# Second half of the embedding projection as the first unit of the kernel, its result kept in DRAM

## The reference

```python
n1 = rmsnorm(h); z = n1 @ w_in                     # q | k | v | u | g_a | g_b
m = sigmoid(g_a) * (attention(q, k, v) @ w_branch_a) + sigmoid(g_b) * (pool(u) @ w_branch_b)
h = h + m @ w_out
h = h + square(relu(rmsnorm(h) @ w_up)) @ w_down
gate = sigmoid(rmsnorm(h) @ w_ple_gate)
e = rmsnorm(p @ w_ple_proj)                         # the embedding: p is 320 x 256, an input
h = h + gate * e
y = rmsnorm(h)
```

## Time and profile before

| | |
|---|---|
| median of the runs | 1684.16 us (1683.98 to 1684.43, three runs) |
| span of the profiled execution | 1682.3 us |
| median less that span | 1.9 us |
| PE busy | 1657.2 us, 99% |
| DVE busy | 853.4 us, 51% |
| ACT busy | 670.3 us, 40% |
| POOL busy | 83.9 us, 5% |
| PE's share of the chain that ended last | 97% |
| moved by DMA | 252.48 MB, mean 150 GB/s |

### The profile page before, as it was taken

One profiled execution on the slowest core, in us unless ns is written; L12 is line 12 of the kernel. 1 busy time (PEld: TensorE's weight loads), 2 busy tenths in 40 slices (PEclk: granted clock), 3 DMA queues, 4 the chain that ended last, 5 costly groups with the idle time before them and its releaser, 6 DMA issues.

```text
span 1682.3 us, 29192 instructions
## 1 busy us (share of the span) xinstructions
PE 1657.2 (99%) x11286; PEld 1649.0 (98%) x11286; DVE 853.4 (51%) x1180; ACT 670.3 (40%) x973; POOL 83.9 (5%) x76
## 2 busy tenths in 40 slices
PE   7999999999999999999999999999999999999996
PEld 7999999999999999999999999999999999999996
DVE  7577544444445556443344443344433544555765
ACT  6355534333333444443334432234333344444442
POOL 3034000000000003000000000000000300000000
PEclk9999999999999999999999999999999999999998
DMA  7533544444444444444444444444444444444431
GB/s 283 172 116 126 198 149 149 149 148 150 149 149 156 150 150 151 150 150 150 150 150 150 150 150 150 149 149 148 146 147 149 148 147 149 144 149 151 147 125 62
DMA packets 37816, 252.48 MB, mean 150 GB/s; under 512 B 5264, under 2 KB 6544, under 8 KB 8336
## 3 DMA queue, kind: packets, MB, share of 16 engines
q1 hardware_dynamic: 35136, 245.59, 41.1%
q10 hardware_dynamic: 2640, 6.35, 1.0%
HBM read 248.65 MB, written 3.27 MB: 150 GB/s over the span
## 4 chain that ended last, share of the span: by engine, by line
PE 97%; DVE 2%; ACT 1%; DMA 0%; issue 0%; POOL 0%; DVEq 0%; SPq 0%; POOLq 0%; ACTq 0%
PE acc L405 32%; PE acc L407 32%; PE acc L406 32%; PE s_ps L457 1%; DVE w_lo L809 0%; DMA h<-in_x 0%; PE o_ps L435 0%; PE t_ps L444 0%; DVE sumsq L874 0%; DVE h L1159 0%; ACT xa_hi L601 0%; DVE xa_lo L865 0%; ACT w_hi L580 0%; POOL prob_t L344 0%; PE m_ps L419 0%
## 5 line engine op out<-in xcount | busy, mean ns | idle before, releaser
L580 ACT ACTIVATE w_hi<-raw 128x1024 fp32r<-128x1024 f32 x462 | 487.4, 1059 | 882.6 <-PE acc L407 878.9
L405 PE MATMUL acc<-xa_hi,w_hi 128*128 128x320 f32 x2112 | 655.5, 310 | 9.4 <-DVE xa_lo L865 9.0
L406 PE MATMUL acc<-xa_lo,w_hi 128*128 128x320 f32 x2112 | 653.3, 309 | 0.0
L407 PE MATMUL acc<-xa_hi,w_lo 128*128 128x320 f32 x2112 | 653.2, 309 | 0.0
L809 DVE TENSOR_TENSOR w_lo<-raw,w_hi 128x1024 fp32r<-128x1024 f32 x462 | 550.6, 1232 | 19.1 <-ACT w_hi L580 18.8
L405 PEld LDWEIGHTS acc<-xa_hi,w_hi 128*128 128x128 f32 x2112 | 397.2, 188 | 10.4 <-DVE w_lo L809 9.6
L406 PEld LDWEIGHTS acc<-xa_lo,w_hi 128*128 128x128 f32 x2112 | 397.2, 188 | 0.2
L407 PEld LDWEIGHTS acc<-xa_hi,w_lo 128*128 128x128 f32 x2112 | 397.1, 188 | 0.0
L405 PE MATMUL acc<-xb_hi,w_hi 128*128 128x320 f32 x1280 | 395.8, 309 | 0.0
L406 PE MATMUL acc<-xb_lo,w_hi 128*128 128x320 f32 x1280 | 395.5, 309 | 0.0
L407 PE MATMUL acc<-xb_hi,w_lo 128*128 128x320 f32 x1280 | 395.5, 309 | 0.0
(11 more groups left out here) (157 smaller groups left out, 938.9 us busy)
## 6 DMA issues: line engine op xcount, KB each, us to landing
raw<-in_weights SPq DMA_DIRECT2D x229, 1024.0 KB, 4.8
h<-in_x SPq DMA_DIRECT2D x4, 640.0 KB, 8.0
h<-in_x ACTq DMA_DIRECT2D x1, 2560.0 KB, 11.2
raw<-in_weights SPq DMA_DIRECT2D x4, 512.0 KB, 9.1
out_y<-h ACTq DMA_DIRECT2D x2, 800.0 KB, 3.5
out_y<-h ACTq DMA_DIRECT2D x1, 640.0 KB, 3.0
bias<-in_alibi SPq DMA_DIRECT2D x1, 512.0 KB, 11.3
p_raw<-in_p_in ACTq DMA_DIRECT2D x1, 320.0 KB, 2.7
```

The source lines that it names most:

```text
L405: nc.tensor.matmul(out, w_hi[:, at:at + P], x_hi[:, m * T:(m + 1) * T], start=k == 0, stop=False)
L406: nc.tensor.matmul(out, w_hi[:, at:at + P], x_lo[:, m * T:(m + 1) * T], start=False, stop=False)
L407: mm = nc.tensor.matmul(out, w_lo[:, at:at + P], x_hi[:, m * T:(m + 1) * T], start=False, stop=k == depth - 1)
L580: nc.scalar.activation(w_hi[:, dst:dst + HALF], raw[:, src:src + HALF], ACT.Copy).then_inc(hi_done, 1)
```

## The change

The unit of embedding chunks 8 to 15 moves from before the last block to the very front; it is called U_FIRST, and all the x units have an index one higher. Its eight chunks go to all eight PSUM banks. DVE evicts the even ones and ACT the odd ones to `e_first`; POOL squares and adds them from there; then SP writes `e_first` to DRAM (`spill`), and ACT reads it back into `e` after the merge. Its weights come in three pieces, p on ACT's queue with the gains behind it. x comes in eight parts instead of four, half of unit 1 after the second part and the other half after the fifth. PE runs eight matmuls on a cleared piece of `w_lo` first. The splits of units 2 and 3 stand after the third and the ninth square.

```diff
-SPLIT_AFTER = (6, 12)
+SPLIT_AFTER = (2, 8)
+U_FIRST = 0
+U_KV = U_FIRST + 1
+X_PARTS = 8
+WARM = 8
+FIRST_PIECES = ((0, HALF // 2), (HALF // 2, HALF), (HALF, UNIT))
...
+        first_bank = (*acc, s_ps, t_ps, o_ps, m_ps)
+        spill = nc.dram_tensor("e_spill", (P, KA * T), F32, kind="Internal").ap()
... SyncE
-            nc.sync.dma_start(g_all[:, :], gains).then_inc(gains_in, 16)
-            load_half(0, 0, first_in[0])
+            for (a, z), done in zip(FIRST_PIECES, (quarter_in, first_in[0], raw_in[0])):
+                load_part(U_FIRST, a, z, done)
             load_x(0)
             load_x(1)
-            load_half(0, 1, raw_in[0])
-            load_x(2)
-            load_x(3)
-            load_half(1, 0, first_in[1])
-            load_half(1, 1, raw_in[1])
-            load(2, 2)
+            load_part(1, 0, HALF, first_in[1])
+            for i in range(2, 5):
+                load_x(i)
+            load_part(1, HALF, UNIT, raw_in[1])
+            for i in range(5, X_PARTS):
+                load_x(i)
+            load(2, stored(2), 2)
...
-            load(3, 3)
+            load(3, stored(3), 3)
+            sp.wait_ge(ev_dve, KA // 2)
+            sp.wait_ge(ev_act, KA // 2)
+            nc.sync.dma_start(spill, e_first[:, :]).then_inc(spilled, 16)
... GpSimd
             nc.gpsimd.memset(odd_sum, 0.0).then_inc(xodd, 1)
+            def embedding_square(n, src, square):
+                if n:
+                    pool.wait_ge(e_add, n)
+                nc.gpsimd.tensor_tensor(square[:, :], src, src, ALU.mult).then_inc(e_s, 1)
+                pool.wait_ge(e_s, n + 1)
+                nc.gpsimd.tensor_tensor(esum[:, :], esum[:, :], square[:, :], ALU.add).then_inc(e_add, 1)
+            pool.wait_ge(ml, 2)
+            for c in range(KA):
+                if c % 2:
+                    pool.wait_ge(ev_act, c // 2 + 1)
+                else:
+                    pool.wait_ge(ev_dve, c // 2 + 1)
+                embedding_square(c, e_first[:, tt(c)], e_sq_first)
             for n in range(KD // 2):
                 pool.wait_ge(xs, 2 * n + 2)
... TensorE
+            pe.wait_ge(warm, 1)
+            for n in range(WARM):
+                mm = nc.tensor.matmul(s_ps[:, :], w_lo[:, 3 * HALF:3 * HALF + P],
+                                      w_lo[:, 3 * HALF:3 * HALF + 512], start=True, stop=True)
+            mm.then_inc(warmed, 1)
+            for t in range(TILES):
+                o, k = divmod(t, KP)
+                if t in (0, TILES // 4, TILES // 2):
+                    pe.wait_ge(lo_done, 4 * t // TILES + 1)
+                if t < KP:
+                    pe.wait_ge(pf_l, k + 1)
+                ... three matmuls of w_hi, w_lo with pf_hi, pf_lo into first_bank[o]
+            pe.wait_ge(ev_dve, 2)
+            pe.wait_ge(ev_act, 2)
...
-            embed(U_P1, C_P1)
... ScalarE
+            for k in range(KP):
+                nc.scalar.dma_start(p_first[:, tt(k)], p_in[:, tt(k)]).then_inc(p_in_first[k], 16)
+            nc.scalar.dma_start(g_all[:, :], gains).then_inc(gains_in, 16)
+            split_first(0)
+            for k in range(KP):
+                act.wait_ge(p_in_first[k], 16)
+                nc.scalar.activation(pf_hi[:, tt(k)], p_first[:, tt(k)], ACT.Copy).then_inc(pf_h, 1)
+            split_first(1)
+            split_first(2)
+            evict_first(1)
             act.wait_ge(gains_in, 16)
+            for c in range(0, 4):
+                high(c)
+            evict_first(3)
+            split(1, 1, [0])
+            evict_first(5)
+            for c in range(4, 8):
+                high(c)
+            evict_first(7)
+            for c in range(8, 10):
+                high(c)
+            split(1, 1, [1])
+            for c in range(10, KD):
+                high(c)
...
+            ahead(U_KV + 1, U_KV + 1)
             act.wait_ge(xl, KD)
...
+            act.wait_ge(spilled, 16)
+            nc.scalar.dma_start(e[:, KA * T:KD * T], spill).then_inc(e_back, 16)
... VectorE
+            nc.vector.memset(w_lo[:, 3 * HALF:3 * HALF + 512].bitcast(F32), 0.0).then_inc(warm, 1)
...
+            split_first(0)
+            for k in range(KP):
+                dve.wait_ge(pf_h, k + 1)
+                nc.vector.tensor_tensor(pf_lo[:, tt(k)], p_first[:, tt(k)], pf_hi[:, tt(k)],
+                                        ALU.subtract).then_inc(pf_l, 1)
+            split_first(1)
+            split_first(2)
+            def evict_first(c):
+                small_ready(dve, used, full, U_FIRST, 0, c)
+                nc.vector.tensor_copy(e_first[:, tt(c)], first_bank[c][:, 0:T]).then_inc(ev_dve, 1)
+            evict_first(0)
+            dve.wait_ge(gains_in, 16)
+            for c in range(0, 4):
+                low(c)
+            evict_first(2)
+            dve.wait_ge(warmed, 1)
+            split(1, 1, [0])
+            evict_first(4)
+            for c in range(4, 8):
+                low(c)
+            evict_first(6)
+            for c in range(8, 10):
+                low(c)
+            split(1, 1, [1])
+            for c in range(10, KD):
+                low(c)
...
-            embed(U_P1, 1)
```

More of the change, by code:

```diff
@@ L86, with stored @@
 C_MLP = C_P0 + KD // 2
-C_P1 = C_MLP + (FB - 1) * 2 * KF
-C_LAST = C_P1 + KD // 2
+C_LAST = C_MLP + (FB - 1) * 2 * KF
 C_GATE = C_LAST + 2 * KF
-assert RAW == 4 and not any(c % BANKS for c in (C_U, C_POOL, C_MIX, C_OUT, C_P0, C_MLP, C_P1, C_LAST, C_GATE))
+assert RAW == 4 and not any(c % BANKS for c in (C_U, C_POOL, C_MIX, C_OUT, C_P0, C_MLP, C_LAST, C_GATE))
+STORED_FIRST = U_LAST - 1
+def stored(u):
+    return STORED_FIRST if u == U_FIRST else u - 1 if u < U_LAST else u
 KX = 3 * CHUNK + SEQ
@@ L167, in encoder_step @@
         vx = h[:, KA * T + NPAIR * KX:KA * T + 2 * NPAIR * KX]
+        with ExitStack() as first:
+            e_first = sb("e_first", KA * T, F32, first)
         with ExitStack() as early:
@@ L374, in _ @@
                     probabilities(U_U - U_STEP - 1 + c)
[L377 to L383, removed]
+            for c in range(KA):
+                pool.wait_ge(taken, C_P0 + c + 1)
+                embedding_square(KA + c, e[:, tt(c)], e_sq)
         @block.tensor
@@ L459, in step @@
                     mm.then_inc(at_qk, 1)
+            pe.wait_ge(warm, 1)
[9 more added lines that the diff above has]
+                    pe.wait_ge(pf_l, k + 1)
+                at = t * P
+                out = first_bank[o][:, 0:T]
+                nc.tensor.matmul(out, w_hi[:, at:at + P], pf_hi[:, k * T:(k + 1) * T], start=k == 0, stop=False)
+                nc.tensor.matmul(out, w_hi[:, at:at + P], pf_lo[:, k * T:(k + 1) * T], start=False, stop=False)
+                mm = nc.tensor.matmul(out, w_lo[:, at:at + P], pf_hi[:, k * T:(k + 1) * T],
+                                      start=False, stop=k == KP - 1)
+                if t % 8 == 7:
+                    mm.then_inc(used, 1)
+                elif k == KP - 1:
+                    mm.then_inc(full, 1)
+            pe.wait_ge(ev_dve, 2)
+            pe.wait_ge(ev_act, 2)
             for u in range(U_KV, U_STEP):
-                unit(u, u % 2, u, u % BANKS, KD, xa_hi, xa_lo,
-                     ready=(lambda o, k: pe.wait_ge(xl, k + 1)) if u == 0 else None)
-                if u == 2:
+                unit(u, u % 2, u - U_KV, (u - U_KV) % BANKS, KD, xa_hi, xa_lo,
+                     ready=(lambda o, k: pe.wait_ge(xl, k + 1)) if u == U_KV else None)
+                if u == U_KV + 2:
+                    pe.wait_ge(ev_act, KA // 2)
                     pe.wait_ge(xadd, KD // 2)
@@ L481, in _ @@
             for u in range(U_STEP, U_POOL):
-                unit(u, u % 2, u, u % BANKS, KD, xa_hi, xa_lo)
+                unit(u, u % 2, u - U_KV, (u - U_KV) % BANKS, KD, xa_hi, xa_lo)
                 step(u - U_STEP)
@@ L617, in _ @@
             root(0, sumsq, r)
-            for u in range(2, U_STEP):
+            for u in range(U_KV + 2, U_STEP):
                 ahead(u, u)
-            act.wait_ge(taken, U_Q)
+            act.wait_ge(e_add, KA)
+            act.wait_ge(taken, U_Q - U_KV)
             act.wait_ge(kv_cache, 32)
@@ L861, in _, with split_first, evict_first, low @@
             dve.wait_ge(ul, 2)
-            split(0, 0, [0])
-            for c in range(KD):
+            def split_first(i):
+                a, z = FIRST_PIECES[i]
+                dve.wait_ge(hi_done, i + 1)
+                nc.vector.tensor_tensor(w_lo[:, a:z], raw[:, a:z], w_hi[:, a:z], ALU.subtract).then_inc(lo_done, 1)
+            split_first(0)
[5 more added lines that the diff above has]
+            split_first(2)
+            def evict_first(c):
+                small_ready(dve, used, full, U_FIRST, 0, c)
+                nc.vector.tensor_copy(e_first[:, tt(c)], first_bank[c][:, 0:T]).then_inc(ev_dve, 1)
+            def low(c):
                 dve.wait_ge(xh, c + 1)
```

102 lines of the change are left out of this document (58 added, 44 removed).

## The result

The changed kernel takes 1692.40 us (median of 4 runs, 1691.63 to 1693.37) against 1684.07 us for the kernel before, measured beside it: a ratio of 1.0049 [1.0037, 1.0061], 8.3 us slower. The profiled execution has a span of 1689.8 us against 1682.3 us, so the traces have 7.5 us to explain. Left out of all ratios are one run of the kernel before (2731.59 us) and one of experiment 5 (3214.82 us), whose mean granted clock was far lower (0.557 and 0.936) than that of the others (0.993 to 0.997).

What follows compares the result with a forecast made beforehand. TensorE was taken to bound the whole, VectorE the first 18 us. U2 at 32.7 - 18.48 before - 7.17 for the moved unit - 0.4 wait + 0.8 clock = +7.4 us: median 1691.6 us, range 1682 to 1696.

Steps and rivals of the forecast that it cites:

- VectorE with GpSimd beside it: From 10.9 us, VectorE's two-SBUF-operand operations alternate with sixteen GpSimd squares and sums: 0.98 us per xa_lo instead of 0.474.
- U2: Start of the second unit on x (index 2 in the changed kernel): 18.48 us before, forecast 32.7, break-even 26.05.
- the head: Kernel start until x can be split: last weight piece landed at 8.2 us, its low part done at 10.5 us.
- rival 1: At xa_lo: VectorE keeps its pace, GpSimd adds less than 1.75 us in all; 1682.3 us, chance 0.15.
- VectorE's chain alone: VectorE's work from 10.5 us to U2 without GpSimd: 13.8 us, putting U2 at 24.3 us.
- rival 2: VectorE reaches U2 at 24.3 us, but late GpSimd sums delay unit 3 to 41 us; 1692.1 us, chance 0.07.
- rival 3: At xa_lo, turns exclude each other for whole instructions: 1.27 us per chunk instead of 0.98; 1696 us, chance 0.06.
- rival 4: At the start, no turns and first weights landing 2 us earlier, U2 at 22 us; 1680 us, chance 0.07.
- The clock: TensorE's clock may fall to 1.2 GHz in its pause before U2: 0.8 us counted, range 0 to 1.6.
- the wait for GpSimd's sum: At the norm's sum: TensorE's 0.4 us wait for GpSimd goes, as the odd sums end near 44 us.
- The first unit's clock: At the start: low clock costs 1.6 us in the first unit, nothing while VectorE opens the next at 16 us.
- After U2: Unit 3 split at 36 to 38 us, odd sums ended near 44; from there the old order, shifted.

Runs made afterwards that it cites:

- experiment 5: Changed kernel, embedding squares and sums on GpSimd waiting until K and V are evicted, weights of U2 split before the squares of x; 1680.09 us, ratio 0.9977.
- Experiment 3: Kernel before, with only sixteen extra GpSimd squares and sums on otherwise unused tiles near the start; 1693.52 us, ratio 1.0056.
- experiment 1: Changed kernel with GpSimd's loop over the embedding moved behind the sums of x and the clearing of q; 1683.29 us, ratio 0.9993.
- experiment 2: Changed kernel with each early GpSimd square and sum replaced by a memset of about its length, which reads nothing; 1681.40 us, ratio 0.9986.
- experiment 4: Changed kernel with dummy TensorE matmuls, 18 before the second half of unit 1 and 14 before U2; 1690.55 us, ratio 1.0039.
- experiment 6: Changed kernel with embedding chunks 0 to 3 squared early and 4 to 7 moved behind the clearing of q; 1687.42 us, ratio 1.0019.
- experiment 7: Changed kernel with dummy matmuls in both pauses and three before each further chunk of unit 1's second half; 1690.20 us, ratio 1.0037.

## Why the prediction was right

**VectorE with GpSimd beside it: right, and the whole of the sign.** U2 was forecast at 32.7 us and came at 32.15. The pair of a square and a sum takes 2.01 us where the row at 647 us gave 1.96. Experiment 3 produces the cost without the change, experiment 1 the change without most of the cost, and experiment 2 shows that GpSimd's reads make it. What it came early is the head: ScalarE began the last piece at 7.51 us and its low part was done at 9.83, not at 10.5. (The working has two slips here that go the other way: 5.89 less 4.6 is 1.29, not 1.1, and 8.2 + 1.19 + 1.22 is 10.61.) From there to U2 it took 22.32 us, where 22.2 were forecast.

**No turns (rival 1)** is what experiments 1 and 2 make by hand: 1683.3 and 1681.4 us, where 1682.3 was worked out; U2 at 24.98 and 23.47 us, where VectorE's chain alone was put at 24.3. Experiment 2 is that chain with the earlier head. Experiment 1 has two things more that the chain left out: the sums of x on GpSimd meet U2's halves, and the first unit at the lower clock holds VectorE for 1.06 us. Experiment 5, with neither and with no square sums before the halves, reaches 22.16. **GpSimd always loses (rival 2)** falls with the 0.84 to 1.04 us of xa_lo. **A whole-instruction lock (rival 3)** would have put the pair near 2.5 us (0.47 + 0.80 twice); it is 2.01. The section of the Trainium skill that the prediction names there gives the exclusive lock for the shared ports in general, and spells "the whole instruction" out for VectorE's two-port modes; for these two-input operations the runs show less than that. **A shorter head (rival 4)** was right in its direction by 0.7 us, not 2.

**The clock was mis-sized.** 0.8 us was counted, half of 1.6; U2 lost 1.53, nearly the upper bound. The reason given, the pause before U2, isn't what the runs point to: in experiment 1 TensorE stands 1.62 us before U2 after a dense stretch and the clock stays, and in experiment 4 it falls in the thin stretch of unit 1 with the pauses filled. But within the longer pause of the changed kernel, 2.95 us, it fell too, and no run keeps the pause of 2.10 us before U2 and fills the thin stretch alone, so that pause's own part stays open.

**The sum's closeness is luck.** It said +7.4, and +7.46 came. Its terms are off by -0.55 us (U2), +0.73 (the clock) and -0.17 (the wait for GpSimd's sum moved the norm's sum by 0.57, the listed 0.41 with the restart), and these cancel: U2 +13.67, the clock +1.53, the wait -0.57 make the +14.63.

**The first unit's clock was counted at nothing, which held only in some executions.** The prediction said that a low clock there costs nothing while VectorE opens the next unit. In experiments 1 and 6 it costs VectorE 1.06 us, by way of ScalarE's first eviction, which stands ahead of the chunks of x. In the changed kernel's profile the first unit ran at 0.147 us a matmul, so nothing of it shows there; the eight warm-up matmuls are the same in all of these.

**After U2: right.** ScalarE split unit 3 at 35.4 to 37.4 us (36 to 38 forecast for its first half), the odd sums of x ended at 42.86 (44), and TensorE waited for neither. The covers named for the edits counted at nothing held: no wait of TensorE for evictions before unit 1, none of ScalarE for the weight load behind the spill, no wait for the read-back, and no change at 1318 us but the missing unit.

The median came out 0.8 us above the forecast, of which the span has 0.1; the profiled execution is the fastest of the four (1691.63 to 1693.37 us), and what sets the others apart isn't shown.

## What to carry to other kernels

GpSimd work that is free under a full TensorE isn't free everywhere: before an early stretch is given to it, look whether VectorE has the path there with two operands in SBUF, and price each GpSimd operation that reads SBUF at one VectorE turn (here about 0.5 us). Put such work where VectorE isn't the limit, or move the wait with it; experiment 5, with the splits in another order as well, turned 8.3 us of loss into 3.9 of gain without touching the unit. And when work that feeds TensorE thins out, count the lower clock of the stretch after it as well.

## What the chip showed beyond that

The granted clock fell here without a long pause: in experiment 4 at about 28.7 us, while TensorE did three matmuls of 0.147 us about once a microsecond and never waited longer than 0.4 us at a time since 20 us. With six matmuls in 0.88 us (experiment 7) it stayed, and it stayed through a pause of 1.62 us after a dense stretch (experiment 1). In the changed kernel it fell at 33.0 us, 0.8 us after U2 had begun without gaps, so the price is paid behind the thin stretch, in the unit that seems to run well. At the very start the column doesn't tell: it shows 1.00 in experiment 1 from 7 to 9 us and in the kernel before from 9 to 12 us, where matmuls come 0.267 us apart; there the pace has to be read from the starts.
